# Score banks in two pairs and three banks for turned weights in a mixer's attention

## What is computed

```python
for layer in range(DEPTH):
    h = rms_norm(x, attn_norm_w[layer])
    proj = h @ w_in[layer]
    a_q, a_i, a_zf, a_zb, a_g, b_u, c_q, c_k, c_v = jnp.split(proj, SPLIT_POINTS, axis=-1)
    o_a = hgrn2_mixer(a_q, a_i, a_zf, a_zb, a_g, lb_all[layer]).astype(x.dtype)
    o_b = fourier_mixer(b_u).astype(x.dtype)
    o_c = dilated_attention_mixer(c_q, c_k, c_v, positions).astype(x.dtype)
    mixed = jnp.concatenate([o_a, o_b, o_c], axis=-1)
    x = x + mixed @ w_out[layer]
...
outs, lses = [], []
for window, dilation in DILATED_PATTERNS:
    o_p, lse_p = dilated_window_attention(q, k, v, window, dilation)
...
weights = jax.nn.softmax(jnp.stack(lses, axis=0), axis=0)
o = jnp.sum(weights[..., None] * jnp.stack(outs, axis=0), axis=0)
```

## Time and profile before

| | |
|---|---|
| timed runs | 2210.08, 2210.2, 2212.2 us, median 2210.2 |
| span of the profiled execution | 2211.8 us |
| TensorE busy | 2148.4 us, 97% |
| VectorE busy | 1324.7 us, 60% |
| ScalarE busy | 949.9 us, 43% |
| GpSimd busy | 189.1 us, 9% |
| attention of layer 0, second scores to the next projection | 197.72 to 257.26 us |
| attention of layer 1, the same | 836.89 to 895.27 us |

### The profile page before, as it was taken

One profiled execution on the slowest core, in us unless ns is written; L12 is line 12 of the kernel. 1 busy time (PEld: TensorE's weight loads), 2 busy tenths in 40 slices (PEclk: granted clock), 3 DMA queues, 4 the chain that ended last, 5 costly groups with the idle time before them and its releaser, 6 DMA issues.

```text
span 2211.8 us, 32932 instructions
## 1 busy us (share of the span) xinstructions
PE 2148.4 (97%) x13984; PEld 1681.6 (76%) x13984; DVE 1324.7 (60%) x1976; ACT 949.9 (43%) x1442; POOL 189.1 (9%) x159
## 2 busy tenths in 40 slices
PE   8998999999999999999999999999999998999997
PEld 6885688888888785788888885676888567777775
DVE  8886555335437867455255453857433454888887
ACT  5445532222234347432223332345221234888885
POOL 1220000000001310100000200000000001122220
PEclk9999999999999999999999999999999998999999
DMA  5222033322222231222222221212110443799985
GB/s 187 69 80 77 20 119 119 119 101 97 102 85 77 72 96 39 76 83 102 102 96 95 96 96 55 77 53 82 59 59 32 144 168 125 292 349 364 358 346 217
DMA packets 55000, 275.69 MB, mean 125 GB/s; under 512 B 13142, under 2 KB 13398, under 8 KB 26048
## 3 DMA queue, kind: packets, MB, share of 16 engines
q1 hardware_dynamic: 45344, 264.32, 33.0%
q0 software_dynamic: 8928, 8.33, 1.1%
q10 hardware_dynamic: 576, 0.87, 0.1%
HBM read 268.31 MB, written 29.36 MB: 135 GB/s over the span
## 4 chain that ended last, share of the span: by engine, by line
PE 86%; DVE 7%; ACT 3%; DMA 1%; issue 1%; SPq 0%; POOL 0%; POOLq 0%; DVEq 0%; ACTq 0%
PE psum L123 83%; PE psum L126 3%; DVE A_mix L136 2%; ACT A_mix L130 1%; DVE WL L136 1%; DMA A_moe<-h_rows,A_moe 1%; ACT A_mix L133 1%; DVE A_second L136 1%; DVE A_mix L156 0%; DVE A_second L144 0%; DVE A_mix L162 0%; ACT WH L130 0%; SPq L168 0%; DMA A_mix<-A_mix 0%; DVE HL L136 0%
## 5 line engine op out<-in xcount | busy, mean ns | idle before, releaser
L136 DVE TENSOR_TENSOR WL<-raw,WH 128x1024 fp32r<-128x1024 f32 x236 | 300.9, 1277 | 351.6 <-ACT WH L130 351.2
L130 ACT ACTIVATE WH<-raw 128x1024 fp32r<-128x1024 f32 x236 | 247.5, 1054 | 357.6 <-PE psum L123 341.7
L123 PE MATMUL psum<-HH,WH 128*128 128x512 f32 x736 | 301.6, 410 | 17.5 <-DVE HL L144 10.1
L123 PE MATMUL psum<-R_op,WH 128*128 128x512 f32 x1024 | 316.0, 390 | 0.0
L123 PE MATMUL psum<-R_ffn,WH 128*128 128x512 f32 x1024 | 315.1, 389 | 0.0
L123 PE MATMUL psum<-HH,WL 128*128 128x512 f32 x736 | 290.3, 394 | 0.0
L123 PE MATMUL psum<-HL,WH 128*128 128x512 f32 x736 | 290.2, 394 | 0.0
L123 PEld LDWEIGHTS psum<-R_op,WH 128*128 128x128 f32 x1024 | 192.2, 188 | 40.6 <-issue 1.0
L123 PEld LDWEIGHTS psum<-R_ffn,WH 128*128 128x128 f32 x1024 | 192.2, 188 | 39.9
L123 PE MATMUL psum<-R_moe 128*128 128x512 f32 x800 | 198.3, 404 | 5.8 <-DVE ring_moe L136 3.4
L123 PE MATMUL psum<-R_ffn,WL 128*128 128x512 f32 x512 | 199.2, 389 | 0.0
(11 more groups left out here) (206 smaller groups left out, 3000.1 us busy)
## 6 DMA issues: line engine op xcount, KB each, us to landing
ring_moe<-in_w_gu SPq DMA_DIRECT2D x64, 1024.0 KB, 10.1
raw<-in_w_in SPq DMA_DIRECT2D x41, 1024.0 KB, 5.0
raw<-in_w_up SPq DMA_DIRECT2D x32, 1024.0 KB, 4.9
raw<-in_w_down SPq DMA_DIRECT2D x32, 1024.0 KB, 4.9
ring_moe<-in_w_dn SPq DMA_DIRECT2D x32, 1024.0 KB, 6.8
raw<-in_w_out SPq DMA_DIRECT2D x12, 1024.0 KB, 4.9
kept<-A_second SPq DMA_DIRECT2D x20, 256.0 KB, 2.6
A_mix<-A_mix SPq DMA_DIRECT2D x64, 64.0 KB, 2.0
```

Of the source, the lines that this page charges most:

```text
L123: return self.raw.matmul(o, l, r, start=start, stop=stop)
L130: return self.raw.activation(o, i, f, scale=scale)
L136: return self.raw.tensor_tensor(o, a, b, op)
```

## The change

Bank numbers become nested: `ATT = ((0, 1), (4, 5)), (2, 3, 6), 7`. Scores of even pairs go to banks 0 and 1, those of odd pairs to 4 and 5; the turned weights go round 2, 3, 6, one bank for each head in turn; values stay in 7. With two pairs of score banks, score(p+1) waits for the row minima of p-1 instead of p, and stands first in its step. The very first use of banks 4 and 5 waits for the recurrence's last read (`rid`, a new mark). turned waits for the copy three banks ago instead of for the same head's copy of the pair before. The latent attention gets `ML_ATT` with one score pair and two turned banks, which are the same banks, waits and order as before.

```diff
-        ATT = (0, 1, 2, 3, 7)
+        ATT = ((0, 1), (4, 5)), (2, 3, 6), 7
+
+        def score_bank(B, p, hh):
+            return bk(B[0][p % len(B[0])][hh])
+
+        def turned_bank(B, p, hh):
+            return bk(B[1][(2 * p + hh) % len(B[1])])
+
+        def before(p, hh, n):
+            return divmod(2 * p + hh - n, 2)
...
-                if p:
-                    e.wait_ge(*at("att_dve", ly, "s", p - 1, 1))
+                if p >= len(B[0]):
+                    e.wait_ge(*at("att_dve", ly, "s", p - len(B[0]), 1))
+                elif p:
+                    e.wait_ge(*at("rec_dve", ly, "rid", 1))
                 else:
                     ready(e)
...
-                    if p:
-                        e.wait_ge(*at("att_act", ly, "pt", p - 1, hh))
+                    if 2 * p + hh >= len(B[1]):
+                        e.wait_ge(*at("att_act", ly, "pt", *before(p, hh, len(B[1]))))
                     e.wait_ge(*at("att_dve", ly, "n", p, hh))
...
             for p in range(19):
+                if p < 15 and len(B[0]) > 1:
+                    score(p + 1)
                 if 2 <= p < 18:
                     turned(p - 2)
                 if p >= 3:
                     values(p - 3)
-                if p < 15:
+                if p < 15 and len(B[0]) == 1:
                     score(p + 1)
                 yield
```

More of the change, by code:

```diff
@@ L1192, in rec_dve @@
                 e.tt(x.oab[hp], x.oab[hp], b, MUL).then_inc(*read("rec_dve", turn, n))
+                mark("rec_dve", ly, "rid", hp)
                 e.wait_ge(*last("rec_dve"))
@@ L1333, in score @@
                 kl = klen(qt)
-                for hh, t in enumerate(scores(e, hp, [bk(B[hh])[:, 0:kl] for hh in range(2)], qt, kl)):
+                for hh, t in enumerate(scores(e, hp, [score_bank(B, p, hh)[:, 0:kl] for hh in range(2)], qt, kl)):
                     t.then_inc(*did("att_pe", ly, "s", p, hh))
@@ L1341, in turned @@
                 for hh in range(2):
-                    if p:
-                        e.wait_ge(*at("att_act", ly, "pt", p - 1, hh))
+                    if 2 * p + hh >= len(B[1]):
+                        e.wait_ge(*at("att_act", ly, "pt", *before(p, hh, len(B[1]))))
                     e.wait_ge(*at("att_dve", ly, "n", p, hh))
                     for k in range(n):
-                        t = e.tr(bk(B[2 + hh])[:, k * 128:(k + 1) * 128], m.Sb[p % 3 * 2 + hh][:, k * 128:(k + 1) * 128], ident)
+                        t = e.tr(turned_bank(B, p, hh)[:, k * 128:(k + 1) * 128], m.Sb[p % 3 * 2 + hh][:, k * 128:(k + 1) * 128], ident)
                     t.then_inc(*did("att_pe", ly, "t", p, hh))
@@ L1357, in values @@
                     for hh in range(2):
-                        o = bk(B[4])[64 * hh:64 * hh + 64, qt * 128:(qt + 1) * 128]
+                        o = bk(B[2])[64 * hh:64 * hh + 64, qt * 128:(qt + 1) * 128]
                         t = e.mm(o, vtok(2 * hp + hh, k), m.PT[p % 2 * 2 + hh][:, k * 128:(k + 1) * 128], k == 0, k == n - 1)
@@ L1390, in att_act @@
                             e.wait_ge(*at("att_pe", ly, "o", p - 4))
-                        e.act(m.PT[p % 2 * 2 + hh][:, 0:kl], bk(B[2 + hh])[:, 0:kl], ACT.Copy).then_inc(
+                        e.act(m.PT[p % 2 * 2 + hh][:, 0:kl], turned_bank(B, p - 2, hh)[:, 0:kl], ACT.Copy).then_inc(
                             *did("att_act", ly, "pt", p - 2, hh))
@@ L1405, in att_dve @@
                             e.wait_ge(*at("att_pe", ly, "t", p - 3, hh))
-                        e.rowmin(m.Sb[p % 3 * 2 + hh][:, 0:kl], bk(B[hh])[:, 0:kl], mask(qt, kl), scale,
+                        e.rowmin(m.Sb[p % 3 * 2 + hh][:, 0:kl], score_bank(B, p, hh)[:, 0:kl], mask(qt, kl), scale,
                                  col(m.ms, p, hh)).then_inc(*did("att_dve", ly, "s", p, hh))
@@ L2044, in build @@
         ML = (3, 4, 5, 6, 7)
+        ML_ATT = ((3, 4),), (5, 6), 7
         def ml_norms():
@@ L2116, in ready @@
                 e.wait_ge(*at("ml_act", "kn", 3))
-            yield from att_pe(e, "ml", scores, lambda h, k: s2.vt[:, k, h * 64:(h + 1) * 64], s2, causal, ready, ML)
+            yield from att_pe(e, "ml", scores, lambda h, k: s2.vt[:, k, h * 64:(h + 1) * 64], s2, causal, ready, ML_ATT)
         def causal(qt):
@@ L2155, in ml_act @@
             yield
-            yield from att_act(e, "ml", s2, causal, lambda e, hp: None, ML)
+            yield from att_act(e, "ml", s2, causal, lambda e, hp: None, ML_ATT)
         def ml_dve(e):
@@ L2202, in mask @@
                 return c("causal")[:, (3 - qt) * 128:512]
-            yield from att_dve(e, "ml", s2, causal, mask, float(-1.0 / np.sqrt(96.0)), evac, ML)
+            yield from att_dve(e, "ml", s2, causal, mask, float(-1.0 / np.sqrt(96.0)), evac, ML_ATT)
         def wide_pe(e, n, y, name, banks, ready):
```

## The result

The changed kernel takes **2199.18 us** (median of 4 runs, 2198.36 to 2199.74); on the same chip the kernel before takes 2210.14 us (4 runs, 2207.72 to 2212.2). The ratio is 0.9949, 95% interval 0.9935 to 0.9963: 11.0 us faster, with 2199.6 us forecast. The profiled execution's span is 2197.9 us, against 2211.8.

The account below looks back on a forecast made before the run. TensorE, with 86% of the span, was taken as the bound, losing time where it waits in the attentions. Gains of 6.8 us (layer 0) and 3.8 (layer 1), together 10.6, turn 2210.2 into 2199.6 us; 8-in-10 range 2197.0 to 2205.5.

Parts of the forecast that it names:

- Step of 3.10 us, no gap in the middle: Middle of both attentions: eight steps without TensorE waiting, 24.80 us instead of 26.97, gain 2.17 us a layer.
- rival A: Evacuation stays 2.20 us after values start, not 1.02; 5.0 us lost, 2204.6 us; chance 0.20 between forecast and it.
- cover of S: Middle, after an evacuation: next scores may go at 3.61 us, TensorE reaches them at 4.12; spare 0.51 us.
- Tail: From values of pair 11 to the attention's end: 9.6 us; gains 3.2 us in layer 0, 1.6 in layer 1.
- Start, layer 0: First steps of layer 0's attention: pair 3's values start at 216.1 instead of 217.51, gain 1.4 us.
- Start, layer 1: First steps of layer 1's attention: TensorE at clock 0.50 is itself the bound, so gain 0.
- rival D: Layer 1's start also at full clock, 1.8 us more, 2197.8 us; inside the forecast's band, which has chance 0.62.
- The waits added on V and the second S: Attention: new waits before values cost 0 to 0.05 us each, 1.4 at most; second scores' wait costs nothing, cover 6.06.
- Rival C: Middle of attention: clock falls, each step at 1.2 GHz costs at most 3.10 us more; slower kernel, chance 0.06.
- B: No measurable change: late evacuation and both tails at half clock, 2.1 us left, 2208.1 us; chance 0.12.

Follow-up runs that it names:

- e4: The kernel before with only the third bank for turned weights added, one pair of score banks, scores last: 2207.27 us, ratio 0.9995.
- e2: The changed kernel with two banks for turned weights instead of three: 2200.14 us, ratio 0.9963 to the kernel before.
- e1: The changed kernel with all its banks, but scores last in a step again: 2206.33 us, ratio 0.9992 to the kernel before.
- e3: The changed kernel with one pair of score banks, scores still first in a step: 2230.42 us, ratio 1.01 to the kernel before.

## Why the prediction was right, step by step

**Step of 3.10 us, no gap in the middle.** Right: 24.86 for 8 steps, with 24.80 forecast, in both layers; gain 2.11 each, 2.17 forecast. No idle note stands before V in the middle. The step of 3.10 was read a little low: V to V is 3.11 in undisturbed steps of both kernels (215.91 to 219.02 here), which makes the 0.06.

**Evacuation soon after V (the rival A).** Right: ScalarE's evacuation in the changed kernel is at 217.06, 1.15 after V(3), and the row minimum follows at 218.29, V + 2.38:

```profile
217.06 0.60 ACT L130 ACTIVATE HH<-psum 128x512 fp32r<-128x512 f32 x1 [0.33 <-PE psum L123]
217.69 0.69 DVE L136 TENSOR_TENSOR HL<-psum,HH 128x512 fp32r<-128x512 f32 x1 [2.20 <-ACT HH L130]
...
218.29 0.68 DVE L162 CUSTOM_DVE_ANT_0 A_mix<-psum,C 128x512 f32<-128x512 f32 x1
```

The sum had 1.02 and 2.25. The 0.13 is what the sum left out: V's passes take 1.09 from start to end, not the 1.02 from group to group, and ScalarE starts 0.06 after that end. It makes the cover of S 4.12 - (2.38 + 1.36) = 0.38 instead of 0.51, which is what the added subtractions found (0.4), and the tail 5.69 + 4 x 1.02 = 9.77 instead of 9.64, rounded to 9.6 (measured 9.72).

**Tail.** Right in layer 1: 1.53, with 1.6 forecast. In layer 0: 3.06, with 3.2 forecast; half of it is the mechanism and half a lower clock that the first trace of before shows and its second does not. The forecast took one trace's clock for the kernel's.

**Start, layer 0.** The time came right, 18.42 us from S(1) to V(3), where 216.1 less 197.72 = 18.38 was forecast, and so did what sets it, ScalarE's copy behind the weight splits. But the forecast took its gain for the change's own at an equal clock, and it is not: of the measured 1.37, 0.9 was the lower clock in the first trace of the kernel before (0.76 on average from 203 to 210), which needs 18.91 at full clock, and the other 0.5 is the third turned bank, as e4 (18.42 with scores last) and e2 (18.90 with scores first) show. That 1.4 was met is in large part luck.

**Start, layer 1.** This is the step that failed: 0 forecast, 1.76 measured (rival D, 1.8). Of the 1.76, 0.50 is the third bank at full clock and 1.26 the clock. The reason given was "the wait that precedes the fall (for the same subtraction) stays". It stays, 1.06 us; what went is most of the pause ahead of it. In the timeline of the kernel before, one more pause stands ahead of the one in the earlier trace rows:

```profile
200.25 1.13 PE L123 MATMUL psum<-A_mix 64*128 64x512 f32 x4 [1.40 <-DVE small L162]
```

1.40 and 1.06 around one S; now a third S stands ahead of the first T, and the pauses are 0.54 and 1.06 (timeline above). In the kernels with scores first and two pairs (8 traces, 16 attention starts) the granted clock was 1.00 at every start. In those with scores last (5 traces, 10 starts, with 2.46 to 2.73 us of pause in all) it fell in 8. Windows of the second trace of before, a start with a fall (layer 0) and one of the two without (layer 1):

```profile
200.00:204.00 4.00, 3.08 (x12) 2.07 (x12) 3.08 (x10) 2.49 (x7) 0.00 (x0) 0.59 0.00 0
...
836.00:843.00 7.00, 5.30 (x40) 3.15 (x40) 6.78 (x24) 5.11 (x12) 0.00 (x0) 1.00 0.00 0
```

So the clock stays up where the scores go first, worth 0.9 to 1.3 us at a start. It goes with the order and not with the banks: all banks with scores last (e1) fell twice, two turned banks with scores first (e2) did not. That the shorter pause is the reason is argued from this count of cases, and was not tried apart from the order. The sum had 10.6 us for the attentions; 11.94 came, 1.76 of it from this term.

**The waits added on V and the second S.** Nothing that can be seen: steps between undisturbed V take 3.11 us with them and without them, so eight of them in the middle leave no room for 0.05 each; S(1) starts with no idle note.

**Rival C, a falling clock in the middle.** Did not come: 1.00 in all windows from 215 to 240 and 842 to 870. The rule of the Trainium skill named there ("TensorE: Matmul & The Clock Gate", section "A second HAM failure mode: psum-queue depth-cycling") would, as the prediction read it, have had the rotation through more banks bring it; these traces disagree with that reading. The kernel of that section also paused often between groups. The changed kernel does not in its middle, so it says nothing of such pauses; the kernel before does, with pauses of 0.38 and 0.29 us at each evacuation, and stood at 1.00 in four middles all the same. The only variant with a lower clock in the middle is the one with pauses of 2.64 us (e3).

**B and the whole.** Two chips give 11.0 and 7.6 us. The attentions' gain is 8.3 us at full clock and 9.3 to 11.9 with the falls that the kernel before showed; the forecast of 10.6 lies within the latter. About 2.5 us of it were the lower clock of one trace, so that the forecast came within 0.4 us on the first chip is luck; on the second it was 3.0 us too large. B did not come: neither evacuation nor tail of the changed kernel was late or at the lower clock.

## What to carry to other kernels

On an engine that runs its list in order, ask first what stands ahead of the one instruction that frees a shared bank: moving the evacuation before two copies gave 1.5 us in each middle and 1.0 in each tail without a bank. The second pair of banks serves to let the scores go first, which brings the same evacuation forward and covers the middle whole. The third bank gives the 0.5 us at the start and 0.5 in the tail. Spare banks without the new order changed the timed runs by less than they can tell (0.9995, 0.9985 to 1.0005, for the third alone), though they shorten the segments. An early evacuation together with the third bank, without the second pair, was not tried. When pauses are summed, look at the pauses just before a wait that stays, since a shorter one went with a clock that stayed up, and count cover from the end of a group's last pass, not from the start of the next group.

## What the runs showed of the hardware

The clock falls of one kernel differ between executions: in the first trace of the kernel before, layer 0's tail ran at 0.50 from 250.7 to 254 after a pause of 1.54 us, in the second it did not, and after the same pause of 1.54 us in e2 it stayed at 1.00 in both layers. Timed runs of one kernel, spread over 8 to 10 us, go roughly with the mean granted clock: 2204.8 us at 0.992 and 2213.4 us at 0.989 for the kernel before, 2198.1 us at 0.994 and 2208.1 us at 0.988 for e2; not strictly, as the changed kernel took 2198.6 us at 0.991 and 2200.5 us at 0.993 on the second chip. A segment of the attention repeats to 0.02 us at full clock, the whole program only to the 8 to 10 us just named; for a change of a few microseconds the segment is the finer measure.
